# Router logits inside the output projection, the norm taken out of the choice, and the gather cut into tiles of 128 slots

## The reference, cut to what matters

```python
h = h + memory_cross_attention(rms_norm(h, norm_cross[l]), mem_n, xa_wq[l], xa_wk[l], xa_wv[l], xa_wo[l])
h = h + hierarchical_moe(rms_norm(h, norm_ffn[l]), moe_router_group[l], moe_router_expert[l],
                         moe_w1[l], moe_w3[l], moe_w2[l])
...
p_group = jax.nn.softmax((xf @ w_rg).astype(F32), axis=-1)
g_idx = jnp.argmax(p_group, axis=-1)
g_gate = jnp.take_along_axis(p_group, g_idx[:, None], axis=-1)
fine = (xf @ w_re).astype(F32).reshape(n, MOE_GROUPS, MOE_PER_GROUP)
fine = jnp.take_along_axis(fine, g_idx[:, None, None], axis=1)[:, 0]
top_v, top_i = lax.top_k(fine, MOE_TOPK)
gate = g_gate * jax.nn.softmax(top_v, axis=-1)
expert = g_idx[:, None].astype(jnp.int32) * MOE_PER_GROUP + top_i.astype(jnp.int32)
...
return (jax.nn.silu(xblk @ w1[e]) * (xblk @ w3[e])) @ w2[e]
```

## Time and profile before

| what | us |
|---|---|
| median of 3 runs | 2020.53 |
| lowest and highest | 2017.41, 2020.79 |
| time of the profiled execution | 2019.82 |
| its span | 2018.0 |
| TensorE busy | 1900.4 (94%) |
| VectorE busy | 832.3 (41%) |
| ScalarE busy | 510.7 (25%) |
| share of the two DMA queues that load weights | 54.4% and 15.2% |

### The profile page before, as it was taken

One profiled execution on the slowest core, in us unless ns is written; L12 is line 12 of the kernel. 1 busy time (PEld: TensorE's weight loads), 2 busy tenths in 40 slices (PEclk: granted clock), 3 DMA queues, 4 the chain that ended last, 5 costly groups with the idle time before them and its releaser, 6 DMA issues.

```text
span 2018.0 us, 25040 instructions
## 1 busy us (share of the span) xinstructions
PE 1900.4 (94%) x10096; PEld 1243.1 (62%) x10096; DVE 832.3 (41%) x1196; ACT 510.7 (25%) x727; POOL 50.9 (3%) x54
## 2 busy tenths in 40 slices
PE   6999999989899999999798999999999999999995
PEld 6898799889777879978653343434443433444332
DVE  4644454788644554335432222322322232223223
ACT  4444343543343434333210000000010000001001
POOL 0000000022310000000000000000000000000000
PEclk9999999999999999999798999999999999999997
DMA  7554445334565454426609999999999999999992
GB/s 275 167 167 146 146 159 175 126 106 146 122 148 169 167 167 163 152 83 188 263 0 419 428 428 430 427 430 427 429 428 429 428 428 429 428 429 427 429 422 99
DMA packets 106973, 556.63 MB, mean 276 GB/s; under 512 B 12336, under 2 KB 12568, under 8 KB 81176
## 3 DMA queue, kind: packets, MB, share of 16 engines
q1 hardware_dynamic: 96952, 423.51, 54.4%
q10 hardware_dynamic: 8928, 130.03, 15.2%
q0 software_dynamic: 1024, 2.10, 1.5%
HBM read 553.51 MB, written 2.10 MB: 275 GB/s over the span
## 4 chain that ended last, share of the span: by engine, by line
PE 79%; DMA 14%; DVE 4%; ACT 2%; issue 1%; SPq 0%; POOL 0%; DVEq 0%; ACTq 0%
PE ps L840 18%; DMA arena<-in_moe_w_dram 13%; PE ps L865 7%; PE ps L851 6%; PE ps L528 6%; PE ps L529 6%; PE ps L530 6%; PE ps L522 6%; PE ps L524 6%; PE ps L523 6%; PE ps L882 3%; PE ps L490 2%; PE ps L812 1%; PE ps L671 1%; DVE w_lo L1338 1%
## 5 line engine op out<-in xcount | busy, mean ns | idle before, releaser
L840 PE MATMUL ps<-arena 128*64 128x512 f32 x2048 | 504.4, 627 | 27.3 <-DMA arena<-in_moe_w_dram 26.9
L1338 DVE TENSOR_TENSOR w_lo<-arena,w_hi 128x1024 fp32r<-128x1024 f32 x264 | 319.3, 1252 | 294.4 <-ACT w_hi L983 293.7
L983 ACT ACTIVATE w_hi<-arena 128x1024 fp32r<-128x1024 f32 x264 | 264.2, 1051 | 333.7 <-PE ps L524 176.0
L840 PEld LDWEIGHTS ps<-arena 128*64 128x64 f32 x2048 | 136.9, 141 | 289.4 <-issue 264.0
L1889 DVE TENSOR_TENSOR arena<-ps,arena 128x1024 f32<-128x1024 f32 x128 | 156.5, 1224 | 222.4 <-PE ps L882 222.4
L865 PE MATMUL ps<-arena 128*64 128x512 f32 x1024 | 229.3, 601 | 0.6 <-DVE arena L1868 0.6
L865 PEld LDWEIGHTS ps<-arena 128*64 128x64 f32 x1024 | 75.4, 142 | 157.3 <-issue 156.6
L522 PE MATMUL ps<-x_hi,w_hi 128*128 128x256 f32 x512 | 146.9, 287 | 6.9 <-DVE w_lo L1338 6.9
L1883 DVE TENSOR_TENSOR d_lo<-ps,d_hi 128x512 fp32r<-128x512 f32 x64 | 41.2, 686 | 264.5 <-ACT d_hi L1236 264.5
L524 PE MATMUL ps<-x_hi,w_lo 128*128 128x256 f32 x512 | 146.0, 285 | 0.0
L523 PE MATMUL ps<-x_lo,w_hi 128*128 128x256 f32 x512 | 146.0, 285 | 0.0
(11 more groups left out here) (347 smaller groups left out, 2682.0 us busy)
## 6 DMA issues: line engine op xcount, KB each, us to landing
arena<-in_moe_w_dram SPq DMA_DIRECT2D x130, 2048.0 KB, 18.5
arena<-in_moe_w_dram ACTq DMA_DIRECT2D x62, 2048.0 KB, 14.1
arena<-in_w_in_dram SPq DMA_DIRECT2D x52, 1024.0 KB, 5.0
arena<-in_xa_wk_dram SPq DMA_DIRECT2D x16, 1024.0 KB, 5.1
arena<-in_xa_wv_dram SPq DMA_DIRECT2D x16, 1024.0 KB, 5.1
arena<-in_w_out_dram SPq DMA_DIRECT2D x16, 1024.0 KB, 5.1
arena<-in_xa_wq_dram SPq DMA_DIRECT2D x16, 1024.0 KB, 5.1
arena<-in_xa_wo_dram SPq DMA_DIRECT2D x16, 1024.0 KB, 5.1
```

Source lines behind the costliest of these rows:

```text
L840: last = mm(ps[rows_, m, :], xe[par][:, ECH * i + c, :], ring_up[m][i][:, c, :], start=(i == 0 and c < 2), stop=(i == ECH - 1 and c >= 2))
L983: fn(hi_ring[(2 * n + u) % 4][:], ring_a[i][:, 2 * u:2 * u + 2, :], ACT.Copy).then_inc(S["w_hi"], 1)
L1338: V.tensor_tensor(w_lo[i][:, 2 * u:2 * u + 2, :], ring_a[i][:, 2 * u:2 * u + 2, :], hi_ring[(2 * n + u) % 4][:].bitcast(F32), ALU.subtract ...
```

## The change: what it does

1. *Logits.* The 16 column blocks of xT are multiplied with the router columns by groups (`logits(n)`), inside the next group's dense products, into one bank. A group is turned after the next group's first chunk, not after its last. The squares are summed by 512 columns (`part_square`).
2. *Norm.* The logits are not scaled before the choice. ScalarE writes h times the norm's factor to hx, and the factor enters the exponentials. The selection holds only zeros and ones.
3. *Choice.* VectorE's steps for the two tokens of a partition and for the two choices are merged (hit01, slot01, e01).
4. *Gather.* Slots are gathered in tiles of 128 (`gather`): the moving operand has 128 columns, the stationary one is as before, taken from hx. Tile 0 is gathered before expert 0, whose tokens VectorE copies straight from the banks (`first_tokens`). Tile 1 comes in two halves between expert 0 and block 1, tiles 2 and 3 in halves in blocks 1 to 4, between the down products and `up(n, 0, 2)`.
5. *Loads.* The router's matrices and constants are loaded in the query projection, and expert 0's up pairs between the last dense groups. SyncE no longer waits for the slot rows ahead of expert 1. The final gain is loaded behind expert 5's pairs.

The core of the diff:

```diff
+            def logits(n):
+                pe.wait_ge(S["tp_act"], n + 1)
+                pe.wait_ge(S["tp_dve"], n + 1)
...
+                for k in range(4 * n, 4 * n + 4):
+                    for j in range(NT):
+                        last = mm(bank(6, NT, 36)[:, j, :], xT[:, k, j * P:(j + 1) * P], wr[:, k, :], start=(k == 0 and j == 0),
+                                  stop=(k == KT - 1), skip_group_check=True)
...
             for n in range(4):
-                dense_split(G_XO + n, False, split[G_XO])
+                dense_split(G_XO + n, False, split[G_XO], part=[0])
                 if n >= 1:
                     group_turned(G_XO, n - 1, turn, 0)
+                dense_split(G_XO + n, False, split[G_XO], part=[1])
+                if n >= 1:
+                    logits(n - 1)
+                dense_split(G_XO + n, False, split[G_XO], part=[2, 3])
...
-            for k_ in range(KT):
...
-                    last = mm(ps[:, 4 + k_ % 4, :], h[:, j, k_::KT], sel_r[:, j, :], start=(j == 0), stop=(j == NT - 1))
...
+            def gather(t, b, at):
+                for c in range(4):
+                    for j in range(NT):
+                        last = mm(ps[:, at, c * P:(c + 1) * P], hx[:, j, 4 * b + c::KT], sel[:, j, t * P:(t + 1) * P],
+                                  start=(j == 0), stop=(j == NT - 1))
...
+            def gather_half(t, half):
...
+                pe.wait_ge(S["g_dve"], 2 * t + half + 2)
+                for b in range(2):
+                    last = gather(t, 2 * half + b, 6 + b)
...
             block_n(0, None, 0)
             slot_rows()
-            block_n(1, 0, 1)
...
+            gather_half(1, 0)
+            gather_half(1, 1)
+            pe.wait_ge(S["tab_dve"], 2)
+            pe.wait_ge(S["g_dve"], 6)
+            block_n(1, 0, 1, (2, 0))
+            block_n(2, 1, 0, (2, 1))
+            block_n(3, 2, 1, (3, 0))
+            block_n(4, 3, 0, (3, 1))
```

On ScalarE and VectorE (the second piece is VectorE's):

```diff
+            act.wait_ge(S["rms_dve"], 1)
             for j in range(NT):
-                step(fn(gexp, logit[:, j, 0:NG], ACT.Exp, bias=negm[:, j:j + 1], accum_out=gsum[:, j:j + 1]))
+                fn(hx[:, j, :], h[:, j, :], ACT.Copy, scale=st[:, 40 + j:41 + j]).then_inc(S["hx_act"], 1)
...
+            def select(a, z):
+                for j in range(NT):
+                    last = V.tensor_scalar(sel[:, j, a:z], iota[:, a:z], slot01[:, j, 0:1], None, ALU.is_equal)
+                step(last)
+                for j in range(NT):
+                    last = V.scalar_tensor_tensor(sel[:, j, a:z], iota[:, a:z], slot01[:, j, 1:2], sel[:, j, a:z], ALU.is_equal, ALU.add)
+                last.then_inc(S["sel_dve"], 1)
```

More of the change, by code:

```diff
@@ L267, in program @@
         gidx8, fidx8 = small(NT, 8).bitcast(U32), small(NT, 8).bitcast(U32)
[L268 to L271, removed]
+        hit01, hit, slots = small(NT, 2 * NE), small(NT, NE), small(NT, NE)
+        hit01 = hit01.rearrange("p j (k e) -> p j k e", k=2)
+        e01, slot01 = small(NT, 2), small(NT, 2)
+        fine4 = small(NT, NG * PG)
+        n_first, n_over, st_first, st_over, st_gap, blocks, blk_in, rtmp = [small(NE) for _ in range(8)]
+        egrp, gsum, ggate, vdif, w0, w1, negm = [small(NT) for _ in range(7)]
         goh4 = small(NT, 4)
@@ L814, in _ @@
[L814 to L827 removed]
+            mm(o_[:, 2, :], ones, hit[:, 0, :], start=True, stop=False)
@@ new lines, in _, with slot_rows @@
+            for b in range(4):
+                gather(0, b, 4 + b).then_inc(S["g_pe"], 1)
+            def gather_half(t, half):
+                if t == 1 and half == 0:
+                    pe.wait_ge(S["sel_dve"], 2)
+                    pe.wait_ge(S["g_act"], 4)
+                pe.wait_ge(S["g_dve"], 2 * t + half + 2)
+                for b in range(2):
+                    last = gather(t, 2 * half + b, 6 + b)
+                last.then_inc(S["g_pe"], 1)
+            def slot_rows():
+                pe.wait_ge(S["g_act"], 4)
+                for k in range(2):
+                    for j in range(NT):
+                        mm(ps[:, 5, (2 * k + j) * P:(2 * k + j + 1) * P], slot01[:, j, k:k + 1].to_broadcast([P, P]), ident[:], start=True, stop=True)
+                pe.wait_ge(S["selg_dve"], 1)
+                for j in range(NT):
+                    last = mm(ps[:, 4, :], onesm, sel_g[:, j, :], start=(j == 0), stop=(j == NT - 1))
@@ L894, in block_n @@
                         down(back, i)
+                if half is not None:
+                    if back >= 1:
+                        pe.wait_ge(S["c_add"], 4 * back)
+                    gather_half(*half)
                 up(n, 0, 2, par)
@@ L898, in block_n @@
                     up(n, 1, i, par)
+                    if half is not None and i == 0:
+                        pe.wait_ge(S["g_dve"], 2 * half[0] + half[1] + 3)
                     if back is not None:
@@ L1773, in _ @@
             step(V.scalar_tensor_tensor(st_gap, st_over, float(-EB), st_first, ALU.add, ALU.subtract))
-            for j in range(NT):
-                rj = rank[:, j, :]
-                step(V.scalar_tensor_tensor(rtmp, rj, float(EB), st_gap, ALU.is_ge, ALU.mult))
-                step(V.tensor_tensor(rtmp, rtmp, rj, ALU.add))
-                step(V.tensor_tensor(rj, rtmp, st_first, ALU.add))
-            slot = rank[:, 0:NT, :]
-            step(V.tensor_tensor(hit0, hit0, slot, ALU.mult))
@@ L1889, in add, with block_n @@
                 V.tensor_tensor(hv, flat(ps[:, b0:b0 + 2, :]), hv, ALU.add).then_inc(S["c_add"], 1)
-            def block_n(back, s_back, par, then):
+            def block_n(back, s_back, par, then, half=None):
                 gating(back, s_back)
@@ L1896, in block_n @@
                 down_lo(back)
+                if half is not None:
+                    gathered(*half)
                 for q in range(4):
```

315 lines of the change are left out of this document (172 added, 143 removed).

## The result

The changed kernel takes 2028.91 us (median of five runs, 2026.99 to 2035.53). The ratio is 1.0045, with a 95% interval of 1.0033 to 1.0057: slower by 0.45%. The forecast was 2024, with a range of 2009 to 2034. Of its three outcomes (faster than 2016.5, same, slower than 2024.5), it is the third, to which the prediction gave 0.44.

What follows compares the result with a forecast made beforehand. The prediction took the expert weight stream to bound the kernel; after the change TensorE bounds until block 5, so the unbroken stream starts at 1204.8 instead of 1200.3: 2019.8 + 4.5 = 2024.3, said as 2024, range 2009 to 2034.

Steps and rivals of the forecast that it cites:

- this case: The prediction's own forecast: 0.22 to 0.24 us a gather record, up to three clock falls, 2018 to 2029 us, chance 0.50.
- dense end to choice: From the dense projection's end to VectorE's start of the choice: about 7.4 us, against 16.84 before.
- The path to the end: The end moves with the moment from which the weight stream runs unbroken and the bytes still ahead of it then.
- Logits: 24 of 32 logit products move ahead of the dense end, 48 records costing 5.6 us, so it comes at 982.4.
- Choice to gather: From the choice's start to the gather's start: 10.25 us, as 6.2 until the ranks are read and 4.05 after.
- The record of the gather: One strided gather product of 128 moving columns: 0.233 us, 256 records in four tiles, 59.7 us in all.
- rival 1: Strided weight loads in the gather overlap fully: 0.1165 us a record, time 1994, chance 0.10; partial form 2013 to 2018, 0.14.
- The pause: Between expert 0's up products and block 1: slot rows, tile 1 in halves with VectorE's copies, table steps, 23.1 us.
- The clock: Granted clock falling to 0.50 after sparse stretches before block 5: 2 us, low end none, high end 10 us.
- rival 3: The clock falls in each gather stretch: 10 us more than none, 2032 us, chance 0.17.
- Sum: Block 5 starts at 1195.9, the unbroken stream at 1204.8, 4.5 us later than before: 2019.8 + 4.5 = 2024.3.
- Rival 2: The weight stream keeps its head start: 41 us gained, time 1979, chance 0.01.

Runs made afterwards that it cites:

- third experiment: The changed kernel with all 32 logit products put back behind the last turn: 2028.98 us, ratio 1.0037.
- the last version: The changed kernel with hx stored contiguously, no pause before block 1, and the sums' weights contiguous too: 1980.12 us, ratio 0.98.

## Why the prediction was right, and where a term was off

The forecast, 2024, missed by 4.9 us, a quarter of a per cent. Its mechanism was the right one: strided weights make the tiles dear, TensorE becomes the bound up to block 5, and the stream's head start is given back. The time lies at the top of the 2018 to 2029 that it gave for this case. That the miss is no larger is in part luck: up to block 5 terms of 9.7 us ran long (first stage 2.5, a turn 1.8, clock 5.4), and terms of about 4.4 us ran short (dense end to choice 0.9, records of the gather 2.4, VectorE's copies and small steps in the pause about 1). By its own steps:

- **The path to the end** held. The stream's head start at its first transfer was 38.3 us (forecast 41), all given back, and what set the time was when block 5 started.
- **Logits, mis-sized.** The dense end was forecast at 982.4 and was 986.74. Of the 4.3 us, 2.5 are the first stage's offset told above. It is not shown to be the change's: executions of kernels built on the changed one began those products at 123.8 to 125.7, and over the first 120 us the granted clock was 0.96 in the changed kernel's trace against 0.99 before. The other 1.8 is a term that I left out. Before, two turns stood ahead of the dense end, and now three do (L483 at 966.77 for 1.78 us is one of them). I counted the logits that move ahead and not the turn that moves with them; behind the dense end I had already taken it away, so the sum was short by one turn. The third experiment shows the other side for the logits: they cost the same wherever they stand. For the turn no run does.
- **Dense end to choice**: forecast 7.4, measured 6.5. **Choice to gather**: 10.25, measured 10.27.
- **The record of the gather**: forecast 0.233, measured 0.222 in tile 0 and 7.18 / 32 = 0.224 in the blocks. The four tiles took 57.3 us instead of 59.7, 2.4 us less. The time hung most on the choice of L851's spacing over the load's duration of 294 ns. That the cost is one of strided weights is shown by the kernels with contiguous hx and with four strides; rival 1 fell with them, since a record costs half only where the stride is 1 or 2.
- **The pause**: forecast 23.1, measured 21.5 (1031.65 to 1053.17). The standstill was 18 us (forecast 20). The prediction says that until 1059 the ring was full and nothing was consumed; by the earlier trace rows expert 0's products used it from 1042.22 on, and what held SyncE last was its wait for the slot rows. No term hangs on this. Block 1 was forecast at 1052.1 and began at 1053.17.
- **The clock, mis-sized.** I put 2 us on it. It stood at 0.50 from 1051.5 for 13.7 us, where the up products of block 1 took 3.68 instead of 1.87 and 3.61 instead of 1.87, and the down products 7.31 instead of 6.87: 4.0 us. Then twice 3.4 us, 1.7 each (3.56 instead of 1.87 at 1133.39 is the first). Another 3.4 us, from 1044.6, lie in the pause and cost about 0.2 there (7.26 instead of 7.08). Together 7.4 us behind the pause: rival 3's direction, and three quarters of its 10 us. What I had not seen is that the pause itself, two half tiles with waits between, precedes the long one: with it and contiguous weights the clock stood at 0.50 for 10.2 us, from 1042.2, and in both kernels without it, strided or not, it fell for 3.4 us at a time only.
- **Sum.** Block 5's up products began at 1201.47, forecast 1195.9: 1.1 from block 1's start and 5.4 of clock, less 1.1 of gather in the blocks; 0.2 is left. With the same 1.3 us from issue to bytes (an estimate), the unbroken stream follows from 1210.6 instead of 1204.8, 5.8 us.
- **The rest of the profiled span** is no part of the change. 2018.0 + 10.3 (1210.6 against 1200.3) makes 2028.3, and the span is 2033.7. A dip of the stream, 323 GB/s from 1970 to 1980 us, is 2.5 of it, and the tail 1.6; 1.3 stay open. Without its late first stage and this dip that execution would take 2030.5, within 1.6 us of the median, 2028.91; as the other executions have no trace, that is argued and not shown. The kernel with late logits is an independent sign: its first stage is as late, its expert 6 went out at 1209.23, its stream has no such dip (429 GB/s from 1970 to 1980), and its profiled execution took 2032.04.
- **Rival 2** (head start kept) would have ended at 1979, and the last version is at 1980, though by another way: its stream, too, slackened before block 1 and ran below its full rate until block 5, and the time came from an earlier block 1 and shorter blocks.

The balance of the change by runs: routing and its loads as changed, with expert 1's load late, 6 us faster (2014.61; norm, merged choice and early loads of the router were not tried apart); that load early, 6.8 more (2007.82); early logits, nothing; the tiles, 21.1 us slower (2028.91). The tiles start the experts earlier and cost 26.3 us more (56.20 against 29.95) of a TensorE that has become the bound there. The idle engine's cheapest repair, the order of hx, gives back 25.5.

## What to carry to other kernels

A gather in small tiles costs its weight loads again in each tile, so look at the stride of the stationary operand before cutting the moving one: a copy that another engine makes anyway can put it side by side, and costs nothing where that engine has slack. A stream that starts earlier is worth only about what the consumer starts earlier; ask when its ring is freed next, and whether the consumer's next blocks are shorter than the transfer of what they use. When a step is moved to the front of a path, count everything that goes with it.

## What the hardware did that I had not expected

- With 128 moving columns and 128x128 fp32 weights, a record costs 0.113 to 0.118 us at a stride of 1 and 2 elements (7.23 us for 64 records at 1, 7.54 at 2) and 0.22 to 0.24 at 4, 8 and 16. The five strides gave two levels and nothing between them.
- Strided records did not feel the clock. With tiles alone, 23 gather records started in 4.8 us at 0.50 (1010.0 to 1014.8) and 24 in 4.8 us at 1.00 (1015.2 to 1020.0); the changed kernel's sums took 3.93 us at 0.50 (1056.85) and 3.88 at 1.00. Contiguous, the sums took 3.61 us at 0.50 (1132.93 in the kernel before with this edit) and 1.93 at 1.00.
- Sixteen such records in a row at stride 4 (3.88 us), with 64 moving columns, were followed by 3.4 us at half clock in four of five blocks of one kernel and in two of the changed kernel's. At stride 1 (1.93 us) the clock stayed at 1.00 for 204 us. It fell again for 13.7 us, from 1211.9, when TensorE had waited 25.7 us for the stream, and in the kernel before with the same edit for 13.7 us, from 1128.0, behind a wait of 25.6. What links sums and falls, no run here tells: the loads and the sums became shorter at once.
- ScalarE's copy of 2048 fp32 a partition with a stride of 16 elements on its read side took 3.73 us instead of 1.99. Its copy from a bank with a stride of 4 took 0.60 us, as without.
